# Twenty-two projection chunks as 512-column matmuls on [high | low] activations, one PSUM bank for each block

## The reference

```python
proj = jnp.einsum("bsd,dn->bsn", h, w_in)                  # block one: 1024 -> 5128 columns
q, k, v, f_logit, g_b, g_c, hc, gate_conv, gate_attn = jnp.split(proj, _SPLITS, axis=-1)
ya = g_b * causal_depthwise_conv(g_c * hc, conv_w)
yb = forgetting_attention(q, k, v, logf)                   # 8 heads of 64
merged = sigmoid(gate_conv) * (ya @ w_branch[0]) + sigmoid(gate_attn) * (yb @ w_branch[1])
...
proj = h @ w_in_2                                          # block two: 1024 -> 3584 columns
rq, rk, rv, rg, dq, dk, dvv = jnp.split(proj, cuts, axis=-1)
ro = silu(rg) * group_norm(retention(rq, rk, rv))          # 4 heads of 128
do = rms_norm(diff_attention(dq, dk, dvv, lam))            # 4 heads, two maps each
out = concatenate([ro, do]) @ w_out
```

## Time and profile before

| | us |
|---|---|
| median of 3 runs | 991.62 |
| lowest, highest | 990.93, 993.40 |
| the profiled execution | 993.32 |
| its span on the core | 991.3 |

### The profile page before, as it was taken

How to read it: one execution, slowest core, us unless ns; L and a number is a source line. 1 busy time by engine, 2 the same in 40 slices (tenths; PEclk the granted TensorE clock), 3 DMA queues, 4 the chain that set the end, 5 groups by cost and what they waited for, 6 DMA issues and landing times.

```text
span 991.3 us, 14456 instructions
## 1 busy us (share of the span) xinstructions
PE 977.9 (99%) x5820; PEld 867.5 (88%) x5820; DVE 677.1 (68%) x686; ACT 498.5 (50%) x660; POOL 16.7 (2%) x20
## 2 busy tenths in 40 slices
PE   9999999999999999999999999999999999999997
PEld 9899999888888888888888888898989888888885
DVE  4547967767777777876767676485664576777776
ACT  5454654773343434834343446474865654343433
POOL 0000000013000000000000000000000000000000
PEclk9999999999999999999999999999999999999998
DMA  7954573564555566555555554634445345656551
GB/s 215 295 164 142 161 272 136 195 207 130 212 178 204 184 197 211 170 173 202 189 185 192 188 184 155 214 113 157 158 141 191 88 167 170 212 169 212 169 170 43
DMA packets 126407, 176.26 MB, mean 178 GB/s; under 512 B 4043, under 2 KB 102557, under 8 KB 126237
## 3 DMA queue, kind: packets, MB, share of 16 engines
q1 hardware_dynamic: 125644, 173.23, 52.8%
q10 hardware_dynamic: 720, 2.43, 0.7%
HBM read 174.60 MB, written 1.05 MB: 177 GB/s over the span
## 4 chain that ended last, share of the span: by engine, by line
PE 89%; DVE 5%; ACT 2%; SPq 2%; issue 1%; DMA 1%; DVEq 0%; ACTq 0%
PE up_banks L572 12%; PE gate_banks L572 12%; PE bank L421 9%; PE bank L422 9%; PE bank L423 9%; PE up_banks L421 7%; PE up_banks L423 7%; PE up_banks L422 7%; PE up_banks L577 6%; PE gate_banks L577 6%; DVE w_lo L1502 2%; SPq L291 1%; ACT w_hi L1004 1%; PE bank L506 1%; DMA stage<-in_w_in 1%
## 5 line engine op out<-in xcount | busy, mean ns | idle before, releaser
L1508 DVE TENSOR_TENSOR w_lo<-stage,w_hi 128x2048 fp32r<-128x2048 f32 x81 | 185.4, 2289 | 96.6 <-ACT w_hi L1011 96.6
L1502 DVE TENSOR_TENSOR w_lo<-stage,w_hi 128x2048 fp32r<-128x2048 f32 x79 | 181.2, 2297 | 90.3 <-ACT w_hi L1004 90.3
L1004 ACT ACTIVATE w_hi<-stage 128x2048 fp32r<-128x2048 f32 x79 | 150.9, 1913 | 75.7 <-PE up_banks L423 47.3
L1011 ACT ACTIVATE w_hi<-stage 128x2048 fp32r<-128x2048 f32 x81 | 152.9, 1904 | 0.0
L421 PE MATMUL up_banks<-act_both,w_hi 128*128 128x256 f32 x480 | 138.7, 289 | 0.6 <-DVE w_lo L1502 0.5
L423 PE MATMUL up_banks<-act_both,w_lo 128*128 128x256 f32 x480 | 136.4, 284 | 0.0
L422 PE MATMUL up_banks<-act_both,w_hi 128*128 128x256 f32 x480 | 136.4, 284 | 0.0
L572 PE MATMUL gate_banks<-act_both,w_hi 128*128 128x512 f32 x528 | 135.4, 393 | 0.0
L572 PE MATMUL up_banks<-act_both,w_hi 128*128 128x512 f32 x528 | 131.7, 391 | 1.2 <-DVE w_lo L1502 1.2
L572 PEld LDWEIGHTS up_banks<-act_both,w_hi 128*128 128x128 f32 x528 | 96.6, 188 | 19.9 <-DVE w_lo L1502 1.4
L572 PEld LDWEIGHTS gate_banks<-act_both,w_hi 128*128 128x128 f32 x528 | 93.8, 189 | 15.8
(11 more groups left out here) (333 smaller groups left out, 1440.2 us busy)
## 6 DMA issues: line engine op xcount, KB each, us to landing
stage<-in_ffn_w SPq DMA_DIRECT2D x66, 1024.0 KB, 5.3
stage<-in_w_in SPq DMA_DIRECT2D x33, 1024.0 KB, 5.3
stage<-in_w_gate_up SPq DMA_DIRECT2D x22, 1024.0 KB, 5.1
stage<-in_w_down SPq DMA_DIRECT2D x11, 1024.0 KB, 5.1
stage<-in_w_out SPq DMA_DIRECT2D x8, 1024.0 KB, 4.9
stage<-in_mem_w_kv SPq DMA_DIRECT2D x8, 1024.0 KB, 5.1
stage<-in_w_branch SPq DMA_DIRECT2D x4, 1024.0 KB, 5.2
stage<-in_mem_w_q SPq DMA_DIRECT2D x4, 1024.0 KB, 5.1
```

The source lines that it names most:

```text
L1004: act.activation(w_hi[:, place, :], stage[:, place, :], copy).then_inc(hi_done, 1)
L1011: act.activation(w_hi[:, place, :], stage[:, place, :], copy).then_inc(hi_done, 1)
L1502: dve.tensor_tensor(w_lo[:, place, :], stage[:, place, :], w_hi[:, place, :].bitcast(F32), ALU.subtract).then_inc(lo_done, 1)
L1508: dve.tensor_tensor(w_lo[:, place, :], stage[:, place, :], w_hi[:, place, :].bitcast(F32), ALU.subtract).then_inc(lo_done, 1)
```

## The change

The 22 chunks in the new list `BLOCKS` (K, GB, GC, HC, GATE_C, GATE_A, RQ, RK, RG) go the way of the feed-forward chunks. Block m of such a chunk has bank m to itself: 8 matmuls of 512 columns and 8 of 256. Before block m TensorE waits until the last content of bank m is read, which for consecutive chunks is block m of chunk c-1. `scaled` becomes three instructions of VectorE: two sums of the halves, one after each block (128 x 512 read, 128 x 256 written), and a multiplication of the result in SBUF. The factors of the chunks Q, DQ, the token-major chunks and all else keep their form. The waits of the readers of a finished chunk go to a new semaphore, `scaled_done`. Core of the diff:

```diff
+BLOCKS = [*range(K, V), *range(GB, BR0), *range(RQ, RV), *range(RG, RG + 2)]
 def through_banks(chunks, first=0):
     for i, c in enumerate(chunks):
-        b = (first + i) % 2
-        BEFORE[c] = next((x for x in reversed(BANK) if BANK[x] == b), None)
-        BANK[c] = b
-        FREED[c] = sum((x in BY_ACT) == (c in BY_ACT) for x in BANK)
+        for key, b in [((c, 0), 0), ((c, 1), 1)] if c in BLOCKS else [(c, (first + i) % 2)]:
+            BEFORE[key] = next((x for x in reversed(BANK) if BANK[x] == b), None)
+            BANK[key] = b
+            FREED[key] = sum((x in BY_ACT) == (key in BY_ACT) for x in BANK)
...
+        def wait_scaled(engine, c):
+
+            engine.wait_ge(scaled_done, BLOCKS.index(c) + 1)
...
+            def up_blocks(c):
+
+
+                pe.wait_ge(lo_done, c + 1)
...
+                for m in range(2):
+                    before = BEFORE[(c, m)]
+                    if isinstance(before, tuple):
+                        pe.wait_ge(up_free, FREED[before])
+                    else:
+                        wait_read(pe, before)
+                    ms = slice(m * P, m * P + P)
+                    for k in range(KD):
+                        pe.matmul(bank[UP + m], wh[:, k, ms], act_both[:, k, :, :].rearrange("p s t -> p (s t)"),
+                                  start=k == 0, stop=False, skip_group_check=True)
+                    for k in range(KD):
+                        mm = pe.matmul(bank[UP + m][:, T:2 * T], wl[:, k, ms], act_hi[:, k, :], start=False, stop=k == KD - 1,
+                                       skip_group_check=True)
+                    if m == 0:
+                        mm.then_inc(block_done, 1)
+                mm.then_inc(used, 1)
...
-            wait_read(pe, RK + 1)
+            wait_scaled(pe, RK + 1)
...
-                wait_read(act, GATE_C + i)
+                wait_scaled(act, GATE_C + i)
...
-                wait_read(act, RG + i)
+                wait_scaled(act, RG + i)
...
             def scaled(c, to, r):
-                dve.tensor_tensor(to, result(c), over(r), ALU.mult).then_inc(up_free, 1)
+
+
+                for m in range(2):
+                    if m == 0:
+                        dve.wait_ge(block_done, BLOCKS.index(c) + 1)
+                    else:
+                        dve.wait_ge(used, c + 1)
+                    dve.tensor_reduce(to[:, m, :], bank[UP + m].rearrange("p (s t) -> p t s", s=2), AX, ALU.add
+                                      ).then_inc(up_free, 1)
+                wait_read(dve, c)
+                dve.tensor_tensor(to, to, over(r), ALU.mult).then_inc(scaled_done, 1)
...
-                wait_read(pool, HC + j)
+                wait_scaled(pool, HC + j)
```

More of the change, by code:

```diff
@@ L221, in build @@
         hi_done, lo_done, used = sem("hi_done"), sem("lo_done"), sem("used")
-        tokens_done = sem("tokens_done")
-        up_free, up_free_act = sem("up_free"), sem("up_free_act")
+        tokens_done, block_done = sem("tokens_done"), sem("block_done")
+        up_free, up_free_act, scaled_done = sem("up_free"), sem("up_free_act"), sem("scaled_done")
         ssq_done, ms_done, std_done, r_done = sem("ssq_done"), sem("ms_done"), sem("std_done"), sem("r_done")
@@ L262, in wait_read @@
         def wait_read(engine, c):
-            engine.wait_ge(up_free_act if c in BY_ACT else up_free, FREED[c])
+            key = (c, 1) if c in BLOCKS else c
+            engine.wait_ge(up_free_act if key in BY_ACT else up_free, FREED[key])
+        def wait_scaled(engine, c):
+            engine.wait_ge(scaled_done, BLOCKS.index(c) + 1)
         def token_result(engine, c, t):
@@ L433, in up_bank_free @@
                     pe.wait_ge(up_read, PAIRS * AFTER_FFN[c] + PAIRS)
+                elif isinstance(BEFORE[c], tuple):
+                    pe.wait_ge(up_free, FREED[BEFORE[c]])
                 elif BEFORE[c] is not None:
@@ L460, in up_product @@
                 mm.then_inc(used, 1)
+            def up_blocks(c):
+                pe.wait_ge(lo_done, c + 1)
+                wh = w_hi[:, c % RING, :].rearrange("p (k n) -> p k n", k=KD)
+                wl = w_lo[:, c % RING, :].rearrange("p (k n) -> p k n", k=KD)
+                for m in range(2):
[14 more added lines that the diff above has]
+                mm.then_inc(used, 1)
             def up(c, hi, lo, ready=None, base=0, between=None):
+                if c in BLOCKS:
+                    up_blocks(c)
+                    return
                 up_bank(c)
```

## The result

The changed kernel takes 1014.34 us (median; 1013.92 to 1015.24) beside 992.51 for the kernel before, run beside it: a ratio of 1.0215, 95% interval 1.0199 to 1.0231, or 21.8 us more. The forecast was 1011.0 in a range of 1004 to 1018. The profiled execution took 1015.24, its span is 1013.3, 22.0 longer than the span of before, so its trace holds the whole difference. The ratios are taken to these, and kernels of different groups are best compared by their ratios.

What follows compares the result with a forecast made beforehand. TensorE, busy 99%, was taken as the bound. K 1.8, GATE 6.6, RQ to RG 8.2 and clock 3.0, savings already set against the waits, made +19.6 us on the median of 991.6: 1011 us, range 1004 to 1018.

Steps and rivals of the forecast that it cites:

- TensorE bounds, and a wait counts in full: Whole kernel: TensorE, busy 99%, sets the end; cuts in its work gain and waits before it lose one for one.
- The saving of 0.165 us a chunk: All 22 changed chunks: larger matmuls save 0.165 us each on TensorE, 3.6 us in all.
- VectorE's sum of 512 numbers at 0.68 us: VectorE's reads of changed chunks: each new sum takes 0.68 us, within 0.61 to 1.22.
- the rival of 1.22 us: VectorE's new sums: 1.22 us each, some 8 us more over the gate and RQ waits, total 1019; chance 5%.
- K: 1.8 predicted: Chunks K and K+1: TensorE stands 3.8 us at K's second block, with a half clock; cost 1.8 us.
- GATE: 9.1 predicted: Gate chunks: 8.9 us of waits, less 1.3 saved, plus 1.5 for the clock: 9.1 us later.
- RQ to RK: 9.7 predicted: From RQ to RK+1: TensorE stands 9.3 us before RK; 8.2 us late plus 1.5 for the clock.
- The clock: Behind the stands of 4.4 and 9.3 us: two half-clock stretches at 1.5 us each, 3.0 us.
- the clock stays: Rival: the waits come but no half clock follows them, 15.8 us lost, 1007; chance 15%.
- every short wait halves the clock: Rival: the four gate waits of 0.8 to 1.45 us cost 1.5 us of clock each, 1017; chance 14%.
- The gain alone, 988: Rival: VectorE answers in time everywhere, no waits, and the 3.6 us gain stays, 988; chance 3%.

Runs made afterwards that it cites:

- fill: Changed kernel with dummy matmuls of 128 columns, 28 ahead of GATE_C+1 and 74 ahead of RK; 1019.22 us, ratio 1.0263.
- fill2: Changed kernel with dummy matmuls of 128 columns, 16 ahead of GATE_C+1 and 40 ahead of RK; 1009.49 us, ratio 1.0177.
- no_k: Changed kernel with chunks K and K+1 put back in the old form; 1012.55 us, ratio 1.0196.
- read_early: Changed kernel with VectorE's read of RQ+1 moved directly behind the maximum, ahead of both differences; 1011.00 us, ratio 1.0177.
- load_only: Kernel before, with two reductions of 512 constants, group numbers 64 apart, added on VectorE behind each of the 22 reads; 1005.21 us, ratio 1.0112.
- plain_only: Kernel before, with the new form for GB, GB+1, GC, GC+1 and HC alone; 991.45 us, ratio 0.9988.

## Why the prediction was right, point by point

- **TensorE bounds, and a wait counts in full.** Right, with 500 us in between without a change (table). That 21.8 us of waits stand beside 22.0 us of time is chance: a wait of 1.58 us behind K went, the matmuls save some 3.3, and the clock costs about 5 more.
- **The saving of 0.165 us a chunk.** About right. From GB's start to GATE_C's the changed kernel needs 39.35 us instead of 40.23, 0.88 for six chunks, 0.15 each; a window over GB and GB+1 is 11.29 long, where the same pair took 11.51. The Trainium skill's 2.5 ns for an instruction ("TensorE: Matmul & The Clock Gate", "Back-to-back issue gap") would give 0.04 a chunk. The Trainium skill has this figure for an isolated matmul and says that in a stream the weight loads count too, so the prediction used it beyond what it is given for. The Trainium skill's own figure for a stream, 131 ns for 512 columns, does not fit here either: these start 0.23 us apart (eight of them from 99.77 to 101.61). I wrote of five chunks ahead of GATE_C; there are six.

```profile
57.52:68.81 11.29, 11.29 (x65) 9.88 (x64) 7.51 (x7) 5.62 (x5) 0.00 (x0) 1.00 0.63 187
```

- **VectorE's sum of 512 numbers at 0.68 us.** Right, so the rival of 1.22 us falls:

```profile
L1612 DVE TENSOR_REDUCE gate<-up_banks 128x256 f32<-128x512 f32 x24 | 15.9, 685 | 9.9 <-PE up_banks L491 9.9
```

- **K: 1.8 predicted, 3.3 found.** The mis-sized term is the stand, 3.8 against 5.48 us. The read of Q+1 that ends it came at 33.01 instead of 31.25, behind a `lo` that waited for a transfer. In the trace SyncE issued that load 1.6 us later (23.12 instead of 21.48): the issues of the parameter rows ahead of it were 0.6 us late, and one of them took 1.40 us instead of 0.30. The four other kernels with K in the new order stood 3.92 to 4.90 us, and the seven with the old form 1.58 to 3.22, so this place moves by a microsecond or so from kernel to kernel, and the changed kernel's trace is the longest of its group. That the change itself delays these issues was not shown.
- **GATE: 9.1 predicted, 9.1 found, by two errors that cancel.** First stand 3.84 (4.4 predicted). The four short ones 1.08, 1.09, 0.42 and 0.76 (1.2, 1.45, 0.8, 1.0): all a little smaller, since the first came out smaller and each half microsecond is handed on. Waits 7.2 instead of 8.9. Against that the clock, 2.4 instead of 1.5. Adding 7.2 and 2.4 and taking off 1.2 to 1.3 for eight chunks leaves 0.7 to 0.8 of the 9.1. The prediction had no term for it: the profile counts a stand from the end of the last matmul, and the next one would have started about 0.16 us ahead of that end (102.56 against 102.72 at the first stand); five stands make 0.8.
- **RQ to RK: 9.7 predicted, 10.3 found.** The stand is 9.09 (9.3 predicted). The half clock cost 2.4 instead of 1.5.
- **The clock: mis-sized by 1.8.** I took 1.5 us from the earlier trace rows, where a half clock of 3.4 us began only 1.0 us after TensorE was back. Behind the longer stands 5.0 and 5.1 us of work ran at half clock, and nearly half of that is lost. fill and fill2 show the cause: with TensorE kept busy both stretches are gone. The size is not a fixed one. Behind the same stand of 3.85 us before GATE_C+1 it was 3.4 us of work in no_k, which is what I had assumed, and 6.2 in read_early:

```profile
104.63:108.00 3.37, 3.37 (x13) 3.02 (x12) 2.50 (x2) 1.86 (x8) 0.00 (x0) 0.50 0.10 11
106.56:112.72 6.16, 6.16 (x19) 5.19 (x20) 4.01 (x4) 3.34 (x14) 0.00 (x0) 0.50 0.25 60
```

  The rival "the clock stays" falls. So does "every short wait halves the clock": behind 1.08, 1.09, 0.42 and 0.76 the rows show 2.06 to 2.08 us for eight matmuls, full clock. The Trainium skill's description, from a bf16 kernel, of a clock that swings when products go through banks in turn ("TensorE: Matmul & The Clock Gate", "A second HAM failure mode: psum-queue depth-cycling") does not fit these four.
- **The gain alone, 988.** Falls; only the plain chunks behave so.
- **The sums cost 1.22 us each, 1019.** Falls with the row of 685 ns above.

The forecast was 3.3 us short of 1014.34. Of that 0.9 is the kernel before, which came out at 992.51 instead of 991.62; the change itself was put at +19.6 and brought 22.0 in the trace, 2.4 more. K gives about 1.5 of these, the clock 1.8 and the time beside each stand 0.8, and smaller stands take back 1.9. The middle of the range was thus met closer than its terms deserve: errors of up to 1.8 us of both signs cancel in part. The mechanism, new waits at the places named, was the measured one.

## To carry to other kernels

When an edit makes a product larger, look first at how many products lie between a bank's use and its next use: here going from two chunks to one cost 17 us of itself, while the extra arithmetic on VectorE, without that, cost 3. Write down, for each bank's release, what stands ahead of the releasing instruction in its engine's queue; the stand before RK was forecast to 0.2 us in this way and that before GATE_C+1 to 0.6, whereas a share of 68% busy told nothing. When a read is moved forward in that queue, follow what it pushes back: 4.3 of 7.6 us returned one step later.

## What was not expected of the hardware

- **The length of a stand does not say whether the clock falls.** It was at 0.50 soon after stands of 1.58 us in the kernel before, and of 2.22 and 2.80 us in load_only, but not after 2.32 us in load_only, 1.90 in plain_only or 3.02 in no_k. Two rows of load_only with their windows, and the one of no_k with its own:

```profile
123.56 1.64 PE L715 MATMUL bank<-const,L 128*128 128x128 f32 x13 [2.32 <-DVE L L1748]
154.09 0.55 PE L422 MATMUL bank<-mix_hi,w_hi 128*128 128x256 f32 x1 [2.22 <-DVE mix_lo L1793]
...
123.81:126.00 2.19, 2.19 (x22) 2.19 (x21) 2.08 (x6) 1.74 (x4) 0.00 (x0) 1.00 0.00 0
154.10:157.00 2.90, 2.90 (x13) 2.90 (x14) 2.90 (x4) 1.34 (x3) 0.00 (x0) 0.50 0.76 304
```

```profile
34.25 0.38 PE L713 MATMUL gate_banks<-small,const 128*128 128x2 f32 x2 [3.02 <-DVE small L1743]
...
35.00:38.00 3.00, 3.00 (x27) 3.00 (x27) 2.12 (x2) 1.01 (x1) 0.00 (x0) 1.00 1.08 281
```

  What decides it was not settled. The stands of 3.84 and 9.09 us brought it; when they were filled with matmuls that nobody needs, it went.
- **The clock differs between executions of one kernel.** Of 43 executions of the kernel before, 21 had a mean granted clock of 0.998 or 0.999 and took 990.5 to 993.0 us, 17 had 0.996 or 0.997 and took 992.2 to 994.6, and 5 had 0.994 and took 995.3 to 995.7. This fits a half clock that follows the same stand in one execution and not in another; a trace was taken of one execution only, so it is not shown. A difference of 1 or 2 us between two kernels needs many executions, or a look at the stretch in the traces.
- **Where the eight numbers of a group lie costs VectorE time in SBUF**: a reduction of 512 numbers took 1.1 us with them 64 apart and 0.68 side by side. The changed kernel's sums of two numbers 256 apart in PSUM took 0.69, so the distance alone does not decide it.
